# Six of sixteen gathered row tiles: gate on ScalarE, sum by accumulating DMA, in the combine of a mixture-of-experts layer

## The chip, the cores and the metric

The kernel is one program on one NeuronCore of a Trainium2 chip. The metric is the device time of one execution in microseconds (us), and the median of several executions is what counts. Five engines run their own instruction streams and meet only at semaphores: TensorE (PE), VectorE (DVE), ScalarE (ACT), GpSimd (POOL) and SyncE (SP). SP, ACT and POOL also issue DMAs.

## What is computed

One encoder layer over 512 tokens of width 1024: a mixer (convolution and neighbourhood attention, added to x to give h), then a mixture of experts, then a final RMSNorm. The change lies in the part of the experts in which their outputs are summed per token. Of the reference this matters:

```python
logits = (xt @ w_router + b_router).astype(jnp.float32)
top_vals, top_idx = lax.top_k(logits, TOP_K)          # TOP_K = 4 of 32 experts
gates = jax.nn.softmax(top_vals, axis=-1)
...                                                    # every expert's block of 128 rows: y
y = y * gate_pad[:, None]
out = jax.ops.segment_sum(y, tok_pad, num_segments=T)
h = h + out
return rmsnorm(h, g_final)
```

So each token's row of h receives four gated rows, one from each of its experts, and the final norm needs the finished row.

## The kernel before

The 512 tokens are four tiles n = 0 to 3 of 128 tokens. h stands in on-chip memory (SBUF) as 128 partitions x 4 tiles x 1024 floats.

The 32 experts run one after the other. An expert has 12 weight pieces of 1 MB (four each for gate, up and down). Each piece is split by ACT (`w_high`) and DVE (`w_low`) into two parts and used by 12 matmuls on PE (two k tiles, two halves, three products). Expert b's 128 output rows go to `y_rows` in DRAM by a DMA that ACT issues in `rows_out`. The last two experts (30 and 31, "late") don't go through DRAM: their gated rows are split into `late_high` (ACT, L849) and `late_low` (DVE, L1456), and PE places them in the four token tiles by one-hot matmuls (`open_tile`, `close_tile`, L1821 to L1833), whose sums stand in PSUM (`pair`).

The rows of the other experts come back as sixteen gathered row tiles, 128 x 1024 floats each. The four rows of a token are sorted by expert, so rank r = 0 is the row of the lowest expert. `row_order` is (r=0, n=0..3) as k = 0 to 3, and then for each n the ranks 1, 2, 3: k = 4 to 6 are tile 0, 7 to 9 tile 1, 10 to 12 tile 2, 13 to 15 tile 3. POOL gathers row tile k by an indirect DMA (L609) into one of nine buffers (`row_buf[k % 9]`), so row tile k of 9 and above waits until DVE has consumed row tile k - 9 (`combined`). DVE waits for the gather (`rows_back`, one of six semaphores) and does h[n] = row * gate + h[n] in one instruction (`add_row`, L1443).

Each engine's order is written out by hand; nothing reorders it:

- DVE in the end: the last weight split (`low_last`, L1206), `late_low` part 0, `add_row` 5 to 8, `late_low` part 1, `add_row` 9 to 15, then `add_late` for the four tiles (L1470: h[n] += PE's sum, after `late_summed`), then, after the norm's factor from POOL, the four final products (L1499).
- ACT in the end: `late_high` part 0, the last weight cast (L818), `late_high` part 1 (after PE's last piece), then the four squares with row sums (L927), each after its `add_late`.
- POOL in the end: the gathers in the order of k, then a branch on an overflow count (no trip is taken with these inputs), then for each tile two small instructions (L551, L553) that give the norm's factor.
- PE in the end: the last down pieces, three `open_tile`, then, after `late_low` part 1, three `close_tile` and tile 3's open and close.
- SP in the end: one output store of 512 KB per tile (L511), each after its final product, and a wait for all four.

Of the kernel before, what the change touches and what calls it, by code (L numbers as in the profile page):

```python
# [10 lines left out]
ALU = mybir.AluOpType  # L11
ACT = mybir.ActivationFunctionType
# [6 lines left out]
NQ = GRID_W // QB  # L19
# [4 lines left out]
N_EXPERTS, TOP_K, D_FF = 32, 4, 1024  # L24
# [17 lines left out]
NJ = NQ * TOP_K  # L42
# [15 lines left out]
def encoder_kernel(nc, x, g_mix, w_in, b_in, conv_w, conv_b, ln_g, ln_b, rpb, w_out, b_out,  # L58
# [3 lines left out]
    with ctx:  # L62
        def sem(name):
            return ctx.enter_context(nc.semaphore(name))
# [16 lines left out]
        def sb(name, shape, dt=F32):  # L81
            return area(name, shape, dt)[0]
# [5 lines left out]
        h = sb("h", [P, NQ, D_MODEL])  # L88
# [104 lines left out]
        row_order = [(0, n) for n in range(NQ)] + [(r, n) for n in range(NQ) for r in range(1, TOP_K)]  # L193
        row_buf = [xg] + [w_raw[i // 2][:, (i % 2) * D_MODEL:(i % 2 + 1) * D_MODEL] for i in range(8)]
        ROW_BUFS, ROW_SEMS = len(row_buf), 6
        y_sb = area_m[:, 1024:2048]
        bias_stage = area_m[:, 3072:4096]
        g_silu = area_t[0:CAP, 0:1024]
# [30 lines left out]
        slot_f, gate_of_rank, gate_extra = (area_t[:, 2128 + NJ * i:2128 + NJ * (i + 1)] for i in (1, 2, 3))  # L229
# [133 lines left out]
        late_high_ready = sem("late_high_ready")  # L363
        late_low_ready = sem("late_low_ready")
        late_summed = sem("late_summed")
        late_added = sem("late_added")
        bias_rows_loaded = sem("bias_rows_loaded")
        bias_high = sem("bias_high")
# [13 lines left out]
        rows_back = [sem(f"rows_back{k}") for k in range(ROW_SEMS)]  # L382
        extra_back = [sem(f"extra_back{n}") for n in range(NQ)]
        extra_added = sem("extra_added")
        combined = sem("combined")
# [130 lines left out]
        def _(pool):  # L516
# [60 lines left out]
            def select_in(e):  # L577
                g.tensor_copy(sel_gate[:, :], is_expert[:, bass.ds(e, 1)].to_broadcast([P, CAP]))  # L578
                g.tensor_copy(sel_up[:, :], is_expert[:, bass.ds(e + N_EXPERTS, 1)].to_broadcast([P, CAP])).then_inc(sel_in_ready, 1)
# [11 lines left out]
            with pool.Fori(0, N_EXPERTS - 2) as j:  # L591
                gather_next(j + 2)
                pool.wait_ge(piece_used, PIECES * j + 8 + UP + 1)
                select_in(j + 2)
            pool.wait_ge(ranks_ready, 1)
            for k, (r, n) in enumerate(row_order):
                if k == 0:
                    pool.wait_ge(y_stored, 16 * (LATE - 1 + 1))
                    pool.wait_ge(xg_transposed, N_EXPERTS)
                elif k < ROW_BUFS:  # L600
                    pool.wait_ge(piece_used, PIECES * (N_EXPERTS - 2) + 8 + GATE + (k - 1) // 2 + 1)
                else:
                    pool.wait_ge(combined, k - ROW_BUFS + 1)
                if k == NQ:
                    pool.wait_ge(y_stored, 16 * (LATE + 1))
                if k >= ROW_SEMS:
                    pool.wait_ge(rows_back[k % ROW_SEMS], 16 * (k // ROW_SEMS))
                i = n * TOP_K + r
                g.indirect_dma_start(out=row_buf[k % ROW_BUFS], out_offset=None, in_=y_rows[0:(LATE if r else LATE - 1) * CAP, :],  # L609
                                     in_offset=bass.IndirectOffsetOnAxis(ap=slot_of_rank[:, i:i + 1], axis=0)).then_inc(rows_back[k % ROW_SEMS], 16)  # L610
            pool.wait_ge(overflow_ready, 2)
            trips = pool.value_load(n_ovf[0:1, 0:1], min_val=0, max_val=MAX_OVERFLOW)
            with pool.If(trips > 0):
# [21 lines left out]
        def _(act):  # L635
            s = nc.scalar
# [94 lines left out]
            for i in range(1, NS + 7):  # L731
# [9 lines left out]
                n = turned_at(i, 2)  # L741
# [9 lines left out]
            for c in range(CC):  # L751
# [3 lines left out]
                             scale=colT[:, 24 + c:25 + c]).then_inc(silu_ready, 1)  # L755
# [82 lines left out]
            def rows_out(b, at, unstored=0):  # L838
# [4 lines left out]
                act.wait_ge(y_ready, b + 1 - unstored)  # L843
                act.dma_start(y_rows[bass.ds(b * CAP, CAP), :], y_sb[0:CAP, :]).then_inc(y_stored, 16)

            def late_high_part(i, at, of):

                act.wait_ge(piece_used, at)
                s.activation(late_high[i][:, :], of[:, :], ACT.Identity, scale=row_gate[:, i:i + 1]).then_inc(late_high_ready, 1)  # L849
# [53 lines left out]
            late_high_part(0, TAIL, pair[2])  # L903
            high_last(3, TAIL + 3)
            act.wait_ge(hT_low_ready, N_EXPERTS)
            late_high_part(1, EXTRA_BASE, pair[0])
            act.wait_ge(overflow_ready, 2)
            trips = act.value_load(n_ovf[0:1, 0:1], min_val=0, max_val=MAX_OVERFLOW)
            with act.If(trips > 0):
# [21 lines left out]
        def _(dve):  # L931
# [182 lines left out]
            for i in range(NS + 6):  # L1114
                n = normalised_at(i, 10)
# [6 lines left out]
                n = turned_at(i, 3)  # L1122
# [334 lines left out]
                                       ALU.mult, ALU.subtract).then_inc(late_low_ready, 1)  # L1457

            late_low_part(0, pair[2])
            for k in range(5, 9):  # L1460
                add_row(k)
            late_low_part(1, pair[0])
            for k in range(9, NJ):
                add_row(k)
            dve.wait_ge(combined, NJ)
            late_sum = [pair[1], pair[2], pair[3], pair[0]]

            def add_late(n):
                dve.wait_ge(late_summed, n + 1)
                v.tensor_tensor(h[:, n, :], h[:, n, :], late_sum[n][:, :], ALU.add).then_inc(late_added, 1)  # L1470

            for n in range(NQ):
                add_late(n)
            trips = dve.value_load(n_ovf[0:1, 0:1], min_val=0, max_val=MAX_OVERFLOW)
            with dve.If(trips > 0):
# [9 lines left out]
                for i in range(NJ):  # L1485
                    n = i // TOP_K
# [395 lines left out]
```

## Time and profile before

| | |
|---|---|
| Median of 3 runs | 1453.19 us (1452.91 to 1456.13) |
| The profiled execution | 1450.85 us |
| Its span, first to last instruction | 1448.9 us |
| PE busy | 1387.8 us (96%) |
| DVE busy | 1270.5 us (88%) |
| ACT busy | 966.5 us (67%) |
| POOL busy | 189.6 us (13%) |
| Mean granted TensorE clock | 0.980 of full speed |

All times "at 1421.79" are microseconds from the start of the span. A line of a timeline has the start, the duration, the engine, the line of the kernel, the operation, output<-input, and a count of instructions merged into the row; in brackets stands the idle time of the engine before it and what ended it. POOLq, SPq and ACTq are the sequencers of these engines, which issue DMAs. "To landing" is the time from the start of a DMA's issue until its semaphore is complete.

### The profile page before, as it was taken

To read this page: it belongs to the slowest core of one execution; us is meant where nothing else is said; L and a number is where in the kernel's file an instruction comes from. 1 tells how busy PE (TensorE), PEld (TensorE's weight loads), DVE (VectorE), ACT (ScalarE), POOL (GpSimd) and SP (SyncE) were. 2 spreads that over 40 slices of the span, in tenths; PEclk is the share of its full clock that TensorE was granted. 3 is DMA by queue.
4 is the path that set the end of the run, shared out by engine and by line. 5 is a ranking of instruction groups with operands and counts; after the bars stand their busy time and mean duration, and the time that the engine had idled before them with its cause. 6 is when DMAs were issued, how large, how long until landed. Compare 5 with 4: busy or idle time off the path is not lost.

```text
span 1448.9 us, 18708 instructions
## 1 busy us (share of the span) xinstructions
PE 1387.8 (96%) x6456; PEld 1146.7 (79%) x6456; DVE 1270.5 (88%) x996; ACT 966.5 (67%) x740; POOL 189.6 (13%) x191
## 2 busy tenths in 40 slices
PE   5999989799999999999999999999999999999994
PEld 4887767678888888888888888888888888888874
DVE  6899855899888888888888888888888888888898
ACT  3132643467777777777777777777777777777761
POOL 3000000011111111111111111111111111111062
PEclk9999789899999999999999999999999999999997
DMA  9922302799999999999999999999999999999983
GB/s 295 337 60 76 128 1 77 271 408 377 384 394 384 383 388 387 374 390 389 373 392 392 385 385 378 382 384 387 385 382 384 388 384 381 397 381 378 404 308 103
DMA packets 84978, 479.55 MB, mean 331 GB/s; under 512 B 10731, under 2 KB 11030, under 8 KB 35798
## 3 DMA queue, kind: packets, MB, share of 16 engines
q1 hardware_dynamic: 71982, 433.40, 76.8%
q0 software_dynamic: 6944, 25.18, 5.0%
q10 hardware_dynamic: 6024, 20.60, 3.6%
q8 instruction: 16, 0.26, 0.1%
q14 instruction: 12, 0.10, 0.0%
HBM read 449.82 MB, written 29.33 MB: 331 GB/s over the span
## 4 chain that ended last, share of the span: by engine, by line
PE 86%; DVE 9%; ACT 1%; issue 1%; DMA 1%; POOL 0%; SPq 0%; POOLq 0%; DVEq 0%; ACTq 0%
PE pair L1747 23%; PE pair L1745 23%; PE pair L1746 23%; DVE area_m L1016 2%; PE pair L1732 2%; PE pair L1725 2%; PE pair L1758 2%; PE pair L1530 2%; PE pair L1531 1%; PE pair L1532 1%; DVE w_low L1170 1%; DVE win_low L991 1%; DVE h L1443 1%; DMA h<-in_x 1%; PE pair L1611 1%
## 5 line engine op out<-in xcount | busy, mean ns | idle before, releaser
L1170 DVE TENSOR_TENSOR w_low<-w_raw,w_high 128x2048 fp32r<-128x2048 f32 x380 | 863.9, 2289 | 108.9 <-ACT w_high L774 105.8
L774 ACT CAST w_high<-w_raw 128x2048 fp32r<-128x2048 f32 x380 | 727.8, 1916 | 279.6 <-PE pair L1747 278.3
L1745 PE MATMUL pair<-w_high,xT_high 128*128 128x512 f32 x1008 | 395.1, 392 | 0.5 <-DVE xT_low L1228 0.5
L1747 PE MATMUL pair<-w_high,xT_low 128*128 128x512 f32 x1008 | 393.0, 390 | 0.0
L1746 PE MATMUL pair<-w_low,xT_high 128*128 128x512 f32 x1008 | 392.4, 389 | 0.0
L1747 PEld LDWEIGHTS pair<-w_high,xT_low 128*128 128x128 f32 x1008 | 189.2, 188 | 39.6
L1745 PEld LDWEIGHTS pair<-w_high,xT_high 128*128 128x128 f32 x1008 | 189.3, 188 | 39.2 <-DVE xT_low L1228 0.9
L1746 PEld LDWEIGHTS pair<-w_low,xT_high 128*128 128x128 f32 x1008 | 189.3, 188 | 38.4
L1745 PE MATMUL pair<-w_high,hT_high 128*128 128x512 f32 x496 | 195.8, 395 | 0.0
L1747 PE MATMUL pair<-w_high,hT_low 128*128 128x512 f32 x496 | 193.3, 390 | 0.0
L1746 PE MATMUL pair<-w_low,hT_high 128*128 128x512 f32 x496 | 193.3, 390 | 0.0
L578 POOL CAST sel_gate<-is_expert 128x128 fp32r (+1 forms) x32 | 34.6, 1082 | 669.3 <-PE pair L1747 669.3
L1747 PEld LDWEIGHTS pair<-w_high,hT_low 128*128 128x128 f32 x496 | 93.1, 188 | 19.6
L1746 PEld LDWEIGHTS pair<-w_low,hT_high 128*128 128x128 f32 x496 | 93.2, 188 | 18.5
L1745 PEld LDWEIGHTS pair<-w_high,hT_high 128*128 128x128 f32 x496 | 93.2, 188 | 18.4
L568 POOL DMA_INDIRECT area_m<-xn_rows,tok_now x32 | 81.4, 2544 | 38.2 <-issue 26.2
L1016 DVE SCALAR_TENSOR_TENSOR area_m<-area_u,convT,area_m 128x512 f32<-128x512 f32 x120 | 83.9, 752 | 0.4
L1532 PE MATMUL pair<-xnT_high,win_low 128*128 128x512 f32 x128 | 50.5, 394 | 0.0
L566 POOL COPY tok_now<-tok_tab 128x1 int32 (+1 forms) x31 | 17.1, 550 | 246.7 <-PE pair L1725 228.9
L1725 PEld LDWEIGHTS pair<-ident,area_m 128*128 128x128 f32 x256 | 33.6, 189 | 8.4 <-DMA area_m<-xn_rows,tok_now 6.0
L551 POOL TENSOR_SCALAR ms<-ss 128x1 f32<-128x1 f32 x12 | 5.8, 482 | 258.5 <-ACT area_t L789 239.7
L1725 PE MATMUL pair<-ident,area_m 128*128 128x128 f32 x256 | 34.3, 278 | 5.5 <-DMA area_m<-xn_rows,tok_now 5.5
(300 smaller groups left out, 1399.6 us busy)
## 6 DMA issues: line engine op xcount, KB each, us to landing
w_raw<-in_w_gate SPq DMA_DIRECT2D x128, 1024.0 KB, 7.0
w_raw<-in_w_up SPq DMA_DIRECT2D x128, 1024.0 KB, 6.5
w_raw<-in_w_down SPq DMA_DIRECT2D x128, 1024.0 KB, 7.0
y_rows<-area_m ACTq DMA_DIRECT2D x30, 512.0 KB, 7.6
ring<-in_w_in SPq DMA_DIRECT2D x5, 2048.0 KB, 17.7
y_rows<-area_t SPq DMA_DIRECT2D x1, 8704.0 KB, 37.0
ring<-in_w_out SPq DMA_DIRECT2D x2, 2048.0 KB, 8.5
h<-in_x SPq DMA_DIRECT2D x4, 512.0 KB, 8.7
```

The costliest lines, as they stand in the source:

```text
L568: g.indirect_dma_start(out=xg[0:CAP, :], out_offset=None, in_=xn2_rows, in_offset=bass.IndirectOffsetOnAxis(ap=tok_now[:, 0:1], axis=0)).t ...
L578: g.tensor_copy(sel_gate[:, :], is_expert[:, bass.ds(e, 1)].to_broadcast([P, CAP]))
L774: s.copy(w_high[:, i % HIGH_RING, :], w_raw[i][:, :]).then_inc(high_ready, 1)
L1016: v.scalar_tensor_tensor(mixedT[:, c, :], u_pad[:, c, k:k + SEQ], convT[:, k * CC + c:k * CC + c + 1], mixedT[:, c, :], ALU.mult, ALU.add) ...
L1170: v.tensor_tensor(w_low[i][:, :], w_raw[i][:, :], w_high[:, i % HIGH_RING, :].bitcast(F32), ALU.subtract).then_inc(low_ready, 1)
L1530: t.matmul(to, a_high, b_high, start=(k == 0 and not opened), stop=False)
L1532: return t.matmul(to, a_low, b_high, start=False, stop=(k == KD - 1))
L1725: last = t.transpose(bank[6 + k // 4][:, (k % 4) * CAP:(k % 4 + 1) * CAP], xg[0:CAP, k::KD], ident[0:CAP, 0:CAP])
L1732: last = t.transpose(bank[6 + k // 4][:, (k % 4) * CAP:(k % 4 + 1) * CAP], h_tok[:, k::KD], ident[0:CAP, 0:CAP])
L1745: t.matmul(to[half], tok_high, hi, start=(opens and kk == 0), stop=False)
L1746: t.matmul(to[half], tok_high, lo, start=False, stop=False)
L1747: last = t.matmul(to[half], tok_low, hi, start=False, stop=(k == KD - 1))
```

## The change

Row tiles k = 10 to 15 (`DMA_ROWS` = 10: ranks 1 to 3 of token tiles 2 and 3) leave DVE. ACT waits for each one's gather and multiplies the buffer by its gates in place (`gate_row_of`); 10 and 11 stand before `late_high` part 1, 12 to 15 behind it. POOL then issues one accumulating DMA for each, from the row buffer into h[n], both in SBUF (`add_by_dma`). The three accumulating DMAs of one tile wait for one another, since each reads and rewrites the same bytes of h. In POOL's order they stand so: gather 13, add 10, gather 14, add 11, gather 15, add 12, add 13, add 14, add 15. On DVE `late_low` part 1 moves ahead of row tile 8, rows 8 and 9 follow it, and the `add_late` of tiles 2 and 3 wait until their three accumulating DMAs have landed.

```diff
+        DMA_ROWS = NQ + 2 * (TOP_K - 1)
...
+        row_gated = sem("row_gated")
+        rows_added = [sem(f"rows_added{n}") for n in range(2)]
...
+            def add_by_dma(k):
+
+                r, n = row_order[k]
+                pool.wait_ge(row_gated, k - DMA_ROWS + 1)
+                if r > 1:
+                    pool.wait_ge(rows_added[n - 2], 16 * (r - 1))
+                pool.dma_start(h[:, n, :], row_buf[k % ROW_BUFS], accum_op=ALU.add).then_inc(rows_added[n - 2], 16)
...
                 g.indirect_dma_start(out=row_buf[k % ROW_BUFS], out_offset=None, in_=y_rows[0:(LATE if r else LATE - 1) * CAP, :],
                                      in_offset=bass.IndirectOffsetOnAxis(ap=slot_of_rank[:, i:i + 1], axis=0)).then_inc(rows_back[k % ROW_SEMS], 16)
+                if k >= DMA_ROWS + TOP_K - 1:
+                    add_by_dma(k - (TOP_K - 1))
+            for k in range(DMA_ROWS + TOP_K - 1, NJ):
+                add_by_dma(k)
             pool.wait_ge(overflow_ready, 2)
...
+            def gate_row_of(k):
+
+                i = row_order[k][1] * TOP_K + row_order[k][0]
+                act.wait_ge(rows_back[k % ROW_SEMS], 16 * (k // ROW_SEMS + 1))
+                s.activation(row_buf[k % ROW_BUFS], row_buf[k % ROW_BUFS], ACT.Identity,
+                             scale=gate_of_rank[:, i:i + 1]).then_inc(row_gated, 1)
...
             act.wait_ge(hT_low_ready, N_EXPERTS)
+            for k in range(DMA_ROWS, DMA_ROWS + 2):
+                gate_row_of(k)
             late_high_part(1, EXTRA_BASE, pair[0])
+            for k in range(DMA_ROWS + 2, NJ):
+                gate_row_of(k)
...
             late_low_part(0, pair[2])
-            for k in range(5, 9):
+            for k in range(5, 8):
                 add_row(k)
             late_low_part(1, pair[0])
-            for k in range(9, NJ):
+            for k in range(8, DMA_ROWS):
                 add_row(k)
-            dve.wait_ge(combined, NJ)
+            dve.wait_ge(combined, DMA_ROWS)
             late_sum = [pair[1], pair[2], pair[3], pair[0]]
 
             def add_late(n):
                 dve.wait_ge(late_summed, n + 1)
+                if n >= 2:
+                    dve.wait_ge(rows_added[n - 2], 16 * (TOP_K - 1))
                 v.tensor_tensor(h[:, n, :], h[:, n, :], late_sum[n][:, :], ALU.add).then_inc(late_added, 1)
```

## Rows read from the trace of the kernel before

**Rows 1.** The page: busy time by engine, and shares of the chain that ended last.
```profile
PE 1387.8 (96%) x6456; PEld 1146.7 (79%) x6456; DVE 1270.5 (88%) x996; ACT 966.5 (67%) x740; POOL 189.6 (13%) x191
...
PE 86%; DVE 9%; ACT 1%; issue 1%; DMA 1%; POOL 0%; SPq 0%; POOLq 0%; DVEq 0%; ACTq 0%
```
**Rows 2.** Timeline of DVE, the tail.
```profile
1411.64 4.51 DVE L1206 TENSOR_TENSOR w_low<-w_raw,w_high 128x2048 fp32r<-128x2048 f32 x2
1416.07 1.28 DVE L1456 SCALAR_TENSOR_TENSOR late_low<-pair,small,late_high 128x1024 fp32r<-128x1024 f32 x1
1417.27 5.44 DVE L1443 SCALAR_TENSOR_TENSOR h<-w_raw,area_t,h 128x1024 f32<-128x1024 f32 x4
1422.94 1.28 DVE L1456 SCALAR_TENSOR_TENSOR late_low<-pair,small,late_high 128x1024 fp32r<-128x1024 f32 x1 [0.24 <-ACT late_high L849]
1424.14 1.27 DVE L1443 SCALAR_TENSOR_TENSOR h<-area_m,area_t,h 128x1024 f32<-128x1024 f32 x1
1425.52 8.23 DVE L1443 SCALAR_TENSOR_TENSOR h<-w_raw,area_t,h 128x1024 f32<-128x1024 f32 x6
1433.78 4.61 DVE L1470 TENSOR_TENSOR h<-h,pair 128x1024 f32<-128x1024 f32 x4
1438.32 2.47 DVE L1499 SCALAR_TENSOR_TENSOR w_raw<-h,rstd,area_a 128x1024 f32<-128x1024 f32 x2
...
1443.23 1.28 DVE L1499 SCALAR_TENSOR_TENSOR w_raw<-h,rstd,area_a 128x1024 f32<-128x1024 f32 x1 [0.72 <-POOL rstd L553]
```
**Rows 3.** Timeline of PE: ends of tile 0's and tile 3's sums.
```profile
1426.29 0.39 PE L1832 MATMUL pair<-late_low,late_1h 128*128 128x512 f32 x1
...
1430.37 0.39 PE L1832 MATMUL pair<-late_low,late_1h 128*128 128x512 f32 x1
```
**Rows 4.** Timeline of ACT, the tail.
```profile
1411.93 1.90 ACT L818 CAST w_high<-w_raw 128x2048 fp32r<-128x2048 f32 x1
1421.79 1.12 ACT L849 ACTIVATE late_high<-pair,small 128x1024 fp32r<-128x1024 f32 x1 [7.96 <-PE pair L1747]
1435.04 1.06 ACT L927 ACTIVATE area_t<-h 128x1024 f32<-128x1024 f32 x1 [12.13 <-DVE h L1470]
...
1438.76 1.06 ACT L927 ACTIVATE area_t<-h 128x1024 f32<-128x1024 f32 x1
```
**Rows 5.** Timeline of POOL: the last three gathers, and the norm factors of tiles 2, 3.
```profile
1411.99 2.74 POOL L609 DMA_INDIRECT w_raw<-y_rows,slot_of_rank  x1 [9.12 <-DVE h L1443]
1418.81 1.93 POOL L609 DMA_INDIRECT w_raw<-y_rows,slot_of_rank  x1 [4.08 <-DVE h L1443]
1421.05 1.08 POOL L609 DMA_INDIRECT w_raw<-y_rows,slot_of_rank  x1 [0.30 <-issue]
...
1438.76 0.89 POOL L551 TENSOR_SCALAR ms<-ss 128x1 f32<-128x1 f32 x1 [0.41 <-ACT area_t L927]
1439.73 1.47 POOL L553 TENSOR_TENSOR rstd<-ms,small 128x1 f32<-128x1 f32 x1
1441.28 1.29 POOL L551 TENSOR_SCALAR ms<-ss 128x1 f32<-128x1 f32 x1
```
**Rows 6.** DMA view, window 1411 to 1418.4 (queue: packets, MB, share of 16 engines; landing).
```profile
q0 software_dynamic: 152, 0.54, 24.1%
...
w_raw<-y_rows,slot_of_rank POOLq DMA_INDIRECT x1, 6.1
```
**Rows 7.** DMA view, windows of the gathers issued at 1418.81 and 1421.05: landing.
```profile
w_raw<-y_rows,slot_of_rank POOLq DMA_INDIRECT x1, 5.1
...
w_raw<-y_rows,slot_of_rank POOLq DMA_INDIRECT x1, 5.5
```
**Rows 8.** Windows view, one stretch: engines busy, clock, DMA share, GB/s.
```profile
1411.50:1412.00 0.50, 0.50 (x3) 0.40 (x3) 0.50 (x2) 0.50 (x2) 0.01 (x1) 1.00 0.00 0
```
**Rows 9.** Landing of all sixteen gathers (L609).
```profile
DMA to landing us min/median/max: 5.0/9.3/13.6
```
**Rows 10.** Landing of the four output stores (L511).
```profile
DMA to landing us min/median/max: 3.7/4.0/4.1
```

## Prediction

> **What bounds the kernel now.** I read the page first: PE is busy for 96% of the span and holds 86% of the chain that ended last [rows 1]. The change touches none of PE's work, so it can pay only after PE's last matmul. I then read the tail engine by engine. PE finishes tile 0's sum at 1426.7 (1426.29 + 0.39) and tile 3's at 1430.76 [rows 3]. DVE is later than that: after `late_high` part 1 (ACT, 1421.79 to 1422.91 [rows 4]) it does `late_low` part 1, then seven rows from 1424.14 to 1433.75, then four `add_late` to 1438.39 [rows 2]. ACT's last square waits for the last of these and starts at 1438.76 [rows 4]; POOL's small instructions follow, slow from 1438.76 on while DVE runs its final products [rows 5]; the last product ends at 1444.51 [rows 2], and its store of about 4.0 us [rows 10] ends the span at 1448.9. So behind PE's last matmul DVE is the bound: tile 3's `add_late` starts at about 1437.2 (start 1433.78, fourth of four at 1.15 us), 6.4 us after its PE sum was there. From its start to the end of the span are 11.7 us. The span is 1448.9, the profiled execution 1450.85, 2.3 us below the median of 1453.19; I add the change in the span to the median.
>
> **What is removed.** Six `add_row` leave DVE. Six took 8.23 us [rows 2], 1.39 us each with the wait between them. With them gone, row 8 and row 9 follow `late_low` part 1 (1424.2) and end at 1426.9; `add_late` of tile 0 can start at once, since PE's sum for it came at 1426.7 [rows 3]. Tile 1 follows at 1428.2. If nothing else held it, tile 3 would start with PE at 1430.9: 6.3 us earlier. That is the whole prize.
>
> **What is added on ACT.** Six activations of a 128x1024 tile. The nearest rows are 1.12 us (from PSUM with a scale) and 1.06 us (from SBUF) [rows 4]; I take 1.1. Gates 10 and 11 stand after the last weight cast, which ends at 1413.83 [rows 4], so they run to about 1416.1. ACT then idled for 7.96 us until 1421.79 [rows 4], so these two are free and `late_high` part 1 isn't late. They need gathers 10 and 11: the DMA engines stand idle at 1411.5 [rows 8] with everything issued before, gather 12 included, landed. Without that cover each would cost 1.1 us of the path through `late_high`. Gates 12 to 15 run from 1422.9, 1.1 us apart, gates 14 and 15 not before their gathers; none is later than the POOL queue needs it, below.
>
> **What is added on POOL and the DMA queue, where the end now hangs.** Write D for the time from the end of an accumulating DMA's issue to its landing. The order on POOL is: gather 13, add 10, gather 14, add 11, gather 15, adds 12 to 15. Adds 11 and 12 wait for the landing of the one before (same tile), 14 and 15 likewise, and 13, although it waits for no add, stands behind 12 in POOL's order. So five landings follow one another on the way to the end: 10, 11 (then 12 and 13 are issued back to back), 13, 14 and 15, and 15 must have landed before tile 3's `add_late`. What is queued behind each waiting add on POOL: gather 14 behind add 10, gather 15 behind add 11, the norm factors of all four tiles behind add 15.
>
> The issue cost: gathers took 2.74 us while DVE ran L1206, 1.93, and 1.08 us [rows 5, 2]. I take 1.9 for add 10 (DVE is busy) and 1.0 for the others, when DVE mostly waits.
>
> D isn't in the trace: there is no accumulating DMA in it, nor any transfer from SBUF to SBUF. Bounds: the same 512 KB as a gather landed 6.1 us after a 2.74 us issue on idle DMA engines, so D = 3.4, and 5.1 - 1.93 = 3.2 for the next; one that went behind another took 5.5 - 1.08 = 4.4 [rows 5 to 7]. That is the lower bound, 3.2, with 1.2 more behind another transfer. An accumulate must read h as well as the row, twice the reading: one gather held all 16 DMA engines for 24.1% of 7.4 us = 1.78 us [rows 6]; the same once more gives D = 5.0. The upper bound is the median gather among weight loads, 9.3 us less a 1.9 us issue, D = 7.4 [rows 5, 9]. I take 5.0, since the engines are otherwise idle there and the second read has to go somewhere.
>
> In sentences that the rest can do without: the Trainium skill (Collectives: The Full Stack, The bandwidth ceiling) says that a reducing transfer is about half as fast as a copy because the add needs two source reads, not because the add itself takes cycles; no transfer in this trace adds, so the trace can't say. 
>
> **The sum**, with D = 5.0 and 0.1 us for a wake:
> - add 10: gate 10 is done at 1415.0, issue 1415.3 to 1417.2, lands 1422.2.
> - gather 14 as before, 1418.81. Add 11: 1422.3 to 1423.3, lands 1428.3. Gather 15 follows: 1423.6 to 1424.9, lands about 1429.7, gate 15 at 1430.9.
> - add 12: 1428.4 to 1429.4, lands 1434.4 (tile 2's `add_late` then, hidden).
> - add 13: 1429.7 to 1430.7, behind add 12 in the queue (+1.2), lands 1436.9.
> - add 14: 1437.0 to 1438.0, lands 1443.0. Add 15: 1443.1 to 1444.1, lands 1449.1.
> - tile 3's `add_late`: 1449.1 to 1450.3. DVE's final products of tiles 0 to 2 stand behind it: to 1454.1. Meanwhile the square ends at 1451.6 and POOL's pair for tile 3 takes between 0.8 and 2.8 us [rows 5]: 1452.5 to 1454.5. POOL's factors for tiles 0 to 2 were done during add 15's flight, which before they were not; that saves some 0.6 us of the 11.7. The last product starts at about 1454.4, ends at 1455.7, and with 4.4 us of store and end as before (1444.51 to 1448.9) the span is 1460.1.
>
> That is 11.2 us more than 1448.9: 1462.05 for the profiled execution, and on the median 1453.2 + 11.2 = **1464.4 us**.
>
> **Rivals.**
> 1. The accumulate costs no more than a copy (D = 3.2). Then add 11 is issued behind gather 14, 1421.05 to 1422.05, lands 1425.3; add 12 to 1427.3 (DVE busy with row 9, 1.9 us), lands 1430.5; add 13 lands at 1433.0, add 14 at 1437.3, add 15 at 1441.6. Tile 3 starts 4.4 us later than now, less 0.6, gives +3.7: 1456.9. With issues of 0.8 us and no queueing behind add 12 it would be about +2.2: 1455.4. For it: landing times are mostly fixed cost (3.2 us against 1.78 us of engine time). Against it: the doubled reading.
> 2. The accumulate is slow, D = 7.4 or more. The same sum gives landings at 1424.6, 1433.1, 1441.6, 1444.1 (13), 1452.6 and 1461.1; +23.2, 1476.4. For it: nothing but that no such transfer is seen; against it: idle DMA engines [rows 8].
> 3. Faster: DVE's relief is collected. The mechanism is a transfer within SBUF, with no DRAM at either end, landing much sooner than a gather. It breaks even where tile 3's last add lands at 1437.8 and gains more than 0.3% where it lands before 1433.4; from add 10's issue end at 1417.2 five links and four issues of 1 us must fit in 16.2 us, so D below about 2.2, against 3.2 for the fastest gather and 3.7 - 0.55 (the store's own issue) for the fastest store [rows 10]. At the limit, PE's 1430.9, the span falls by 6.3 + 0.6 us: 1446.3.
> 4. The edit does nothing to the end because another wait hides it: ACT's gates make `late_high` late, or the adds of both tiles run side by side. The first is excluded by 7.96 us of idle; the second by POOL's order. What is left of it is case 1.
>
> **How the numbers follow.** Chances: forecast (D between about 3.7 and 6.5, +4.5 to +19) 0.58; rival 1, 0.22; rival 2, 0.15; faster, 0.04; no effect by another way, 0.01. A measurement of this kernel tells about 0.3% (4.4 us) from no change. Rival 1 is mostly just within that, so: slower 0.78, same 0.18, faster 0.04. The range takes in rival 1's copy-priced sum and reaches to D = 7.4: 1455.5 to 1477.
>
> **What would show it.** In the changed kernel's trace: no `add_row` after about 1427 and DVE idle before the `add_late` of tile 2 and, longest, of tile 3; PE unchanged to 1430.8 (if PE's end moves, my reading of ACT's idle time is wrong); POOL idle four or five times for several us, each ended by the landing of an accumulating DMA; their landing from the start of issue near 6 us (4.2 if rival 1 holds, 8.4 or more if rival 2); the q0 queue's engine time up by six transfers of about 3.5 us. After the last landing some 11 us to the end. The prediction is wrong if adds land within 3 us of their issue, if tile 3's chain doesn't start behind tile 2's last issue, or if the landing isn't what ends DVE's wait.

## The result and the profile after

The changed kernel takes 1461.27 us (median of 6 runs, 1460.64 to 1462.83) against 1453.05 us (6 runs, 1451.91 to 1456.13) of the kernel before, measured together: a ratio of 1.0053 with a 95% interval of 1.0040 to 1.0066, 8.2 us slower. The forecast was 1464.4 us in a range of 1455.5 to 1477.

The profiled execution's span is 1459.0 us, 10.1 us over that of before. The page of the changed kernel, busy time by engine, where [rows 1] stood: PE's work is the same, DVE has six instructions less, ACT and POOL six more each.

```profile
PE 1387.9 (95%) x6456; PEld 1146.3 (79%) x6456; DVE 1263.1 (87%) x990; ACT 972.6 (67%) x746; POOL 193.6 (13%) x197
```

The timeline of DVE in the tail answers [rows 2] (line numbers have moved: L1469 is `add_row`, L1482 `late_low`, L1498 `add_late`, L1527 the final products).

```profile
1424.68 1.28 DVE L1482 SCALAR_TENSOR_TENSOR late_low<-pair,small,late_high 128x1024 fp32r<-128x1024 f32 x1 [1.56 <-ACT late_high L871]
1425.88 1.27 DVE L1469 SCALAR_TENSOR_TENSOR h<-w_raw,area_t,h 128x1024 f32<-128x1024 f32 x1
1427.26 1.28 DVE L1469 SCALAR_TENSOR_TENSOR h<-area_m,area_t,h 128x1024 f32<-128x1024 f32 x1
1428.58 2.35 DVE L1498 TENSOR_TENSOR h<-h,pair 128x1024 f32<-128x1024 f32 x2
1434.74 1.22 DVE L1498 TENSOR_TENSOR h<-h,pair 128x1024 f32<-128x1024 f32 x1 [3.80 <-DMA h<-w_raw]
1447.34 1.22 DVE L1498 TENSOR_TENSOR h<-h,pair 128x1024 f32<-128x1024 f32 x1 [11.38 <-DMA h<-w_raw]
1448.58 3.68 DVE L1527 SCALAR_TENSOR_TENSOR w_raw<-h,rstd,area_a 128x1024 f32<-128x1024 f32 x3
1452.69 1.28 DVE L1527 SCALAR_TENSOR_TENSOR w_raw<-h,rstd,area_a 128x1024 f32<-128x1024 f32 x1 [0.44 <-POOL rstd L556]
```

DVE is done with its rows at 1428.5, does `add_late` of tiles 0 and 1, and then stands idle for 3.80 us before tile 2's and 11.38 us before tile 3's, each time until an accumulating DMA into h has landed. The 8.2 us that six `add_row` took are off DVE, and 15.2 us of waiting have come in. Who makes DVE wait stands in POOL's timeline (L604 is the accumulating DMA, L620 the gather; it answers [rows 5]).

```profile
1412.61 2.74 POOL L620 DMA_INDIRECT w_raw<-y_rows,slot_of_rank  x1 [9.89 <-DVE h L1469]
1416.98 1.00 POOL L604 DMA_DIRECT2D h<-w_raw  x1 [1.63 <-ACT w_raw L865]
1420.62 2.03 POOL L620 DMA_INDIRECT w_raw<-y_rows,slot_of_rank  x1 [2.64 <-DVE h L1469]
1422.61 1.01 POOL L604 DMA_DIRECT2D h<-w_raw  x1
1423.93 1.03 POOL L620 DMA_INDIRECT w_raw<-y_rows,slot_of_rank  x1 [0.30 <-issue]
1429.16 1.88 POOL L604 DMA_DIRECT2D h<-w_raw  x2 [4.21 <-DMA h<-w_raw]
1437.63 0.87 POOL L604 DMA_DIRECT2D h<-w_raw  x1 [6.60 <-DMA h<-w_raw]
1442.70 0.87 POOL L604 DMA_DIRECT2D h<-w_raw  x1 [4.21 <-DMA h<-w_raw]
```

Add 10 goes at 1416.98, add 11 at 1422.61, 12 and 13 back to back at 1429.16, 14 at 1437.63, 15 at 1442.70. Three of these waits end with the landing of an add: 12 waits for 11, 14 for 13, 15 for 14. The chain that ended last, in order of time (start, duration, what), is in its last 25 us before the tail nothing but these landings:

```profile
1422.61 5.99 DMA h<-w_raw
...
1429.76 7.33 DMA h<-w_raw
...
1437.63 4.54 DMA h<-w_raw
...
1442.70 4.55 DMA h<-w_raw
...
1447.34 1.23 DVE h L1498
```

The last two stand alone on the queue: 4.54 and 4.55 us from the start of the issue to the landing. The 7.33 us are add 13's, which was issued 0.6 us behind add 12, while that one was under way.

**Why the two profiles differ by 10.1 us and the medians by 8.2.** PE's last matmul starts at 1432.17 in the changed kernel, 1.8 us later than [rows 3] has it. The granted clock makes up most of it (1.6 us), and the rest was there at the start of the experts. The windows view (engines busy, then the granted clock, DMA share, GB/s), one line of before, then two of the changed kernel:

```profile
1406.00:1408.00 2.00, 2.00 (x11) 1.64 (x10) 1.55 (x2) 2.00 (x2) 0.00 (x0) 1.00 1.02 410
```

```profile
1404.00:1406.00 2.00, 1.65 (x9) 1.65 (x10) 2.00 (x2) 0.00 (x0) 0.00 (x0) 0.72 0.98 393
1406.00:1408.00 2.00, 2.00 (x6) 1.52 (x6) 1.44 (x2) 2.00 (x2) 0.00 (x0) 0.50 1.03 408
```

In both, PE has been idle for 2.8 us before it goes on at 1404.2 and 1404.4. In the profile of before the clock then stayed at 1.00 (2.4 GHz), in that of the changed kernel it fell to 0.50 (1.2 GHz) for some 3.5 us. From the last weight cast on ACT before that idle time to `late_high` part 1 are 23.0 us in before and 24.6 us in the changed kernel. The change isn't what makes it fall. The second profile of the order with two chains (below) has all six accumulating DMAs and a clock that stays at 1.00 behind the same idle time, with 22.9 us for the same distance:

```profile
1408.00:1410.00 2.00, 2.00 (x13) 1.74 (x13) 1.89 (x2) 1.33 (x2) 0.23 (x1) 1.00 1.01 416
```

The profiles of the other ten runs below show the fall and 24.4 to 24.6 us, two of them of kernels without any of the six DMAs. So that neither the start nor the clock touches them, the experiments are read by a distance: from the start of `late_high` part 1 on ACT (it starts with PE's last piece) to the start of tile 3's `add_late` on DVE. Before: 1421.79 to 1437.2, 15.4 us [rows 2, 4]. Changed: 1423.53 to 1447.34, 23.8 us. The difference, 8.4 us, agrees with the 8.2 us of the medians.

### The profile page after: what moved, and what is told of

Read it like the earlier page. It is cut to its first block, busy times and chain, and to the rows that moved or that the text cites. A ratio compares the mean times of both kernels' runs of the same rounds, so it can differ in the third digit from the quotient of the medians.

```text
span 1459.0 us, 18714 instructions
## 1 busy us (share of the span) xinstructions
PE 1387.9 (95%) x6456; PEld 1146.3 (79%) x6456; DVE 1263.1 (87%) x990; ACT 972.6 (67%) x746; POOL 193.6 (13%) x197
## 4 chain that ended last, share of the span: by engine, by line
PE 81%; DVE 9%; SPq 4%; DMA 3%; issue 1%; ACT 1%; POOL 0%; POOLq 0%; DVEq 0%; ACTq 0%
PE pair L1775 23%; PE pair L1773 23%; PE pair L1774 23%; DVE area_m L1042 3%; SPq L457 2%; PE pair L1760 2%; PE pair L1753 2%; PE pair L1786 2%; DMA h<-w_raw 2%; DVE w_low L1196 1%; SPq L447 1%; DMA h<-in_x 1%; DVE win_low L1017 1%; PE pair L1639 1%; DVE ring L1063 1%
## 5 line engine op out<-in xcount | busy, mean ns | idle before, releaser
L1773 PEld LDWEIGHTS pair<-w_high,hT_high 128*128 128x128 f32 x496 | 93.7, 189 | 18.5
L1774 PEld LDWEIGHTS pair<-w_low,hT_high 128*128 128x128 f32 x496 | 93.5, 189 | 18.6
L1370 DVE SCALAR_TENSOR_TENSOR area_q<-area_t,area_q 128x1024 f32<-128x1024 f32 x32 | 38.9, 1217 | 0.1
```

Source lines behind the costliest of these rows:

```text
L1370: v.scalar_tensor_tensor(h_tok, g_silu, SILU_TOP, u_lim, ALU.min, ALU.mult).then_inc(h_tok_ready, 1)
L1773: t.matmul(to[half], tok_high, hi, start=(opens and kk == 0), stop=False)
L1774: t.matmul(to[half], tok_high, lo, start=False, stop=False)
```

## The experiments

The theory: the end hangs on accumulating DMAs that wait for one another, each landing some 4.5 us or more (five in a row by the forecast; the chain shows four, 11, 13, 14 and 15); ACT's gates and the reordering on DVE cost nothing. The rivals: the cost is in the bytes or the load on the queue, in ACT's gates, in DVE's new order, or in contention.

### A plain copy in place of the accumulate

```diff
-                pool.dma_start(h[:, n, :], row_buf[k % ROW_BUFS], accum_op=ALU.add).then_inc(rows_added[n - 2], 16)
+                pool.dma_start(h[:, n, :], row_buf[k % ROW_BUFS]).then_inc(rows_added[n - 2], 16)
```

> The changed kernel with the six accumulating DMAs made plain copies: h's tiles 2 and 3 are overwritten by the gated row, so the sum over a token's four rows is left out there. Order, waits and bytes of the row buffers stay. Theory (five landings in a row set the end, and an accumulate is dearer than a copy because it reads h as well): in the changed kernel's trace a lone accumulate took 4.54 us from the start of its issue to its landing, of which the DMA engines moved data for about 2.8 us; a gather of the same bytes held them 1.8 us. A copy should land in about 3.6 us, 0.9 to 1.0 us sooner, and with five links the span should fall by 4.5 to 5 us: +3 to +4 us over the kernel before. Rival (fixed cost of issue and landing, the reading doesn't matter): landing stays at 4.5 us and the time at +8 us.

Measured: 1456.98 us against 1453.33, ratio 1.0024 (1.0014 to 1.0034), +3.6 us. A lone copy lands in 2.88 us, sooner than the 3.6 us expected. The DMA view of the window around the lone transfer of add 14 (queue: packets, MB, share of 16 engines; landing), first the accumulate in the changed kernel (window of 4.9 us), then the copy (3.4 us):

```profile
q0 software_dynamic: 144, 0.52, 56.4%
...
h<-w_raw POOLq DMA_DIRECT2D x1, 512.0 KB, 4.5
```

```profile
q0 software_dynamic: 144, 0.52, 38.0%
...
h<-w_raw POOLq DMA_DIRECT2D x1, 512.0 KB, 2.9
```

The accumulate holds the 16 engines for 56.4% of 4.9 = 2.76 us, the copy for 38.0% of 3.4 = 1.29 us: 2.1 times as long for the same bytes. The issue is shorter too, 0.54 against 0.87 us. So the accumulation is part of a link's price. The Trainium skill (Collectives: The Full Stack, The bandwidth ceiling) says of the reducing step of a collective that it is half as fast as a copy because the add needs two source reads. The ratio of 2.1 agrees, though these runs can't tell the second read from the addition itself.

That the time came out as expected is in part luck. The two lone links shortened by 1.66 us each, add 11's and 13's by 0.8 and 1.0, together 5.1 us. Copy 13, issued behind copy 12, still took 6.29 us to land. In its last 2.9 us the queue moved hardly anything (window 1432.8 to 1435.7):

```profile
q0 software_dynamic: 15, 0.05, 5.0%
```

What holds up the last packets of a transfer issued right behind another stays open.

### Half the columns

```diff
-                pool.dma_start(h[:, n, :], row_buf[k % ROW_BUFS], accum_op=ALU.add).then_inc(rows_added[n - 2], 16)
+                pool.dma_start(h[:, n, 0:HALF], row_buf[k % ROW_BUFS][:, 0:HALF], accum_op=ALU.add).then_inc(rows_added[n - 2], 16)
```

> The changed kernel with the accumulating DMAs on columns 0 to 511 only: the additions of the other half of the columns are left out for these six row tiles. Theory (each link is a fixed part of about 1.8 us, issue included, and 2.8 us of moving data that halves with the bytes): a lone link falls from 4.54 us to about 3.2 us, five links by 6.5 to 7 us, so the time is +1 to +2 us over before. Rival (fixed cost per descriptor or per DMA): links stay above 4.2 us and the time at +7 us or more. If DVE's or PE's own tail took over as the bound, the fall would stop at about -1 us relative to before; it should not come to that.

Measured: 1455.76 us, ratio 1.0013 (1.0003 to 1.0023), +2.4 us; a lone link takes 3.30 us. 256 KB less save 1.24 us, so, if the time goes in a straight line with the bytes, a link of 4.54 us is 2.5 us that go with them and 2.1 us that don't. The lone link came out as expected. The total is 0.4 to 1.4 us above it because five links were counted, and the chain has four. The timeline of POOL:

```profile
1422.86 1.02 POOL L604 DMA_DIRECT2D h<-w_raw  x1
1424.17 1.03 POOL L620 DMA_INDIRECT w_raw<-y_rows,slot_of_rank  x1 [0.30 <-issue]
1428.32 1.87 POOL L604 DMA_DIRECT2D h<-w_raw  x2 [3.11 <-ACT w_raw L865]
```

From add 11's issue to add 12's are 5.5 us, against 6.6 in the changed kernel: 1.1 us less. (The row names ACT as the releaser, but gate 12 was done by 1426.0; by the kernel's waits it was add 11's landing, which is under way together with gather 15 at its full size.) Add 13's landing falls from 7.33 to 5.59 us. With 1.24 us for each of the two lone links the sum is 1.1 + 1.7 + 2.5 = 5.3 us, and the distance from `late_high` to `add_late` falls by as much.

### ACT's gates alone

```diff
+            for k in range(DMA_ROWS, DMA_ROWS + 2):
+                gate_row_of(k)
             late_high_part(1, EXTRA_BASE, pair[0])
+            for k in range(DMA_ROWS + 2, NJ):
+                gate_row_of(k)
...
+                if k >= DMA_ROWS:
+                    dve.wait_ge(row_gated, k - DMA_ROWS + 1)
+                    v.tensor_tensor(h[:, n, :], row_buf[k % ROW_BUFS], h[:, n, :], ALU.add).then_inc(combined, 1)
+                    return
```

> The kernel before with ScalarE's part of the change alone: ACT multiplies row tiles 10 to 15 by their gates, DVE then adds them with a plain add instead of multiply and add. Theory (ACT's part is hidden in its 8 us of idle time and only the DMAs cost): DVE's six adds keep the 1.28 us or fall to 1.2 us each, the time is -0.5 to 0 us of before, and late_high part 1 starts where PE's last piece ends. Rival (the gates hold up late_high part 1 or arrive later than DVE wants them): the time rises by 1 to 3 us, with DVE idle ahead of its adds.

Measured: 1452.46 us, ratio 0.9989 (0.9979 to 0.9999), -0.9 us. ACT's timeline:

```profile
1415.96 2.20 ACT L852 ACTIVATE w_raw<-w_raw,area_t 128x1024 f32<-128x1024 f32 x2
1423.97 1.12 ACT L858 ACTIVATE late_high<-pair,small 128x1024 fp32r<-128x1024 f32 x1 [5.81 <-PE pair L1764]
```

The first two gates take 2.2 us of ACT's idle time, and 5.81 us of it are left before `late_high`, which still waits for PE. The gates are free, and DVE's plain adds come at a pitch of 1.30 instead of 1.37 us.

### DVE's new order alone

```diff
-            for k in range(5, 9):
+            for k in range(5, 8):
                 add_row(k)
             late_low_part(1, pair[0])
-            for k in range(9, NJ):
+            for k in range(8, NJ):
                 add_row(k)
```

> The kernel before with the one step of the change that moves no work: VectorE does late_low part 1 ahead of row tile 8. Theory (the reordering is neutral for the end, since DVE does the same instructions and is the bound behind PE's last matmul): DVE waits about 1.5 us for late_high part 1 with row 8 not yet done, so up to 1.4 us later at the end, 0 to +1.5 us. In the changed kernel that wait is harmless, since its end hangs on the DMAs. Its trace also shows whether TensorE's granted clock falls after the 2.8 us gap at 1401 to 1404 in a kernel with no accumulating DMA: if it does, the 1.6 us by which all later work was late in the changed kernel's profile is no effect of the change; the rival is that only kernels with the change show it.

Measured: 1454.11 us against 1453.56, ratio 1.0009 (0.9998 to 1.0020): no difference that can be told, and in the trace the distance from `late_high` to `add_late` is 1.4 us longer, from the 1.62 us that DVE waits for `late_high`. Its windows view shows the fall of the clock (0.59 over these 2 us) with no accumulating DMA in the kernel:

```profile
1406.00:1408.00 2.00, 2.00 (x7) 1.57 (x7) 1.08 (x2) 1.88 (x2) 0.00 (x0) 0.59 1.02 404
```

### Two chains side by side

The six row tiles are taken as rank 1 of tiles 2 and 3, rank 2 of both, rank 3 of both. The bytes are the same, but each chain has three links and they run beside each other.

```diff
-        row_order = [(0, n) for n in range(NQ)] + [(r, n) for n in range(NQ) for r in range(1, TOP_K)]
+        row_order = [(0, n) for n in range(NQ)] + [(r, n) for n in range(2) for r in range(1, TOP_K)] + [(r, n) for r in range(1, TOP_K) for n in (2, 3)]
```

> The changed kernel with the last six row tiles taken in the order rank 1 of tiles 2 and 3, rank 2 of both, rank 3 of both, so that each accumulate waits for the one before the last and the two tiles' chains run side by side. The same six transfers and bytes. Theory (serial landings cost, not bytes): by the links measured, adds 10 to 15 land at about 1421, 1426, 1430, 1432, 1435.5 and 1438.5 on the time axis of the kernel before, the last add_late starts some 1 to 2 us later than before, and the time is +0.5 to +2.5 us over before, 6 to 7 us better than the change. Rival (the cost is the load on the DMA queue or on SBUF, since the bytes are the same): as the change, +8 us. Second rival (tile 3's chain now starts early but gather 15, held behind add 11, arrives late): gather 15 lands after 1429 and the last add waits for its gate, +4 us.

Measured: 1458.71 us (7 runs), ratio 1.0031 (1.0018 to 1.0044), +5.4 us: above what was expected, while the distance in the trace (1423.11 to 1441.22 = 18.1 us) said +2.7. So both kernels were measured once more, together.

> The two-chain order once more, since its first measurement (+2.6 to +6.4 us over before) was above what was expected of it and didn't agree with its own profiled execution (span +2.8 us once the late PE is taken off). Theory A (serial landings only, the first estimate): +0.5 to +2.5 us. Theory B (landings side by side lengthen each other, since both transfers want all 16 DMA engines; links of 5.0 to 7.0 us in its chain of work instead of 4.5 us): +3 to +5 us, still 3 to 5 us under the change. Rival (bytes alone count): the same as the change.

> The changed kernel itself, beside the two-chain order on the same chip, so that the two are compared with the same runs of before. Theory: +7 to +9 us over before, as on the first measurement; the lone accumulates of tile 3 take 4.5 us again. A drift of the chip would show here as another distance.

Measured: the two chains 1455.83 us (11 runs) against 1453.94, ratio 1.0014 (1.0005 to 1.0023), +1.9 us; the changed kernel 1461.92, ratio 1.0058 (1.0046 to 1.0071), +8.0 us as before. The second distance of the two chains is 18.3 us (1425.05 to 1443.38), +2.9. The intervals of the two measurements overlap only at 1.0018 to 1.0023; I take the traces' +2.8 us.

The traces show one thing that can part two measurements so far. The stream of experts doesn't start at the same time in every execution. Before any changed instruction, the first ACT cast of `xT_high` behind 335 us starts at 336.2 in the first profile of the two chains (1455.16 us) and at 339.6 in the second (1457.24 us). Of the first measurement's seven executions three lie at 1455.2 to 1455.7 and four at 1458.7 to 1460.5. Whether those four started late isn't shown, since only the profiled one has a trace.

Either way the same six transfers in another order cost 2 to 5 us and not 8, so neither bytes nor load on the queue make the change's loss; the rival falls. The chain that ended last of the second profile:

```profile
1418.50 5.44 DMA h<-w_raw
...
1424.13 6.23 DMA h<-w_raw
...
1430.91 6.99 DMA h<-w_raw
...
1438.43 4.86 DMA h<-w_raw
```

Side by side a link takes 5 to 7 us instead of 4.5: what is gained by fewer links is partly lost again. That is what the first estimate had left out; between the two theories of the second run the measurement doesn't decide (+1.9 is nearer the first, the links are the second's).

### One tile by DMA

Tile 2 alone goes by DMA, DVE takes row tiles 13 to 15 again.

```diff
-            for k in range(DMA_ROWS + TOP_K - 1, NJ):
-                add_by_dma(k)
...
-            for k in range(8, DMA_ROWS):
+            for k in (8, 9, 13, 14, 15):
                 add_row(k)
```

> The changed kernel with tile 2 alone by accumulating DMA (row tiles 10 to 12); VectorE takes 13 to 15 again. Theory (a chain of landings costs nothing while it ends before DVE's own rows): three links, the last landing at about 1433 on the axis of before; DVE's rows end 4.2 us earlier than before at 1429.6, its add_late of tile 2 waits 1 us for the landing, tile 3's starts 3 us earlier than before. Time -1.5 to -3.5 us. Rival (accumulating DMAs cost in themselves, by contention with DVE's or ACT's accesses to SBUF): instructions of DVE get longer and the time is no better than before.

Measured: 1451.02 us, -2.5 us by the medians, ratio 0.9990 (0.9979 to 1.0002), which just includes no change; the distance in the trace is 2.7 us shorter. In that trace three links cost DVE no wait at all:

```profile
1428.56 4.06 DVE L1466 SCALAR_TENSOR_TENSOR h<-w_raw,area_t,h 128x1024 f32<-128x1024 f32 x3
1432.65 4.61 DVE L1495 TENSOR_TENSOR h<-h,pair 128x1024 f32<-128x1024 f32 x4
```

DVE goes from its last row straight into four `add_late`, at the durations it has without such DMAs (4.06 for three rows, 1.28 each). Add 12 is issued at 1429.35 and is under way beside these rows. So here an accumulating DMA doesn't slow DVE; it costs only when somebody waits.

### One row of each tile, early

If a landing costs only where it is waited for, the rows for the DMAs should be ones whose landing nobody needs: rank 1 of tiles 1, 2 and 3, one link each. They are gathered as k = 5 to 7, ACT gates them in its idle time ahead of `xT_high` (4.7 us before), and POOL issues them behind gather 12, when it idled for 9.1 us until gather 13 [rows 5].

```diff
+                if k == ROW_BUFS + NQ - 1:
+                    for t in range(1, NQ):
+                        pool.wait_ge(row_gated, t)
+                        pool.dma_start(h[:, t, :], row_buf[NQ + t], accum_op=ALU.add).then_inc(rows_added[t], 16)
...
                     if last and i == DOWN + 2:
+                        for k in range(NQ + 1, 2 * NQ):
+                            gate_row_of(k)
                         hT_high_part(N_EXPERTS - 1, xT_high)
...
+                if r == 2 and n:
+                    dve.wait_ge(rows_added[n], 16)
```

> A new arrangement: three row tiles by ScalarE and accumulating DMA, but one each of tiles 1, 2 and 3 (rank 1), gathered as k = 5 to 7, gated in ACT's idle time at 1401 to 1405, added while POOL idles before gather 13, so that no add waits for another and all are down before VectorE comes to these tiles. Theory (what costs is a landing that somebody waits for): VectorE's tail is three rows of 1.39 us shorter, nobody waits for an add; last add_late 4 us earlier, time -3 to -4.5 us: about 1449.5. Rival (beside weight loads the adds take 8 to 12 us and gather 14 and 15, which now wait for the adds' buffers, come late; or the gates hold up ACT's xT_high and so PE): time within 1 us of before or worse.

Measured: 1449.17 us against 1453.56, ratio 0.9974 (0.9962 to 0.9985), -4.4 us. The adds land only after 11.9 to 13.7 us, beside weight loads and gathers, and nobody waits for them:

```profile
DMA to landing us min/median/max: 11.9/13.3/13.7
```

```profile
1426.63 5.43 DVE L1462 SCALAR_TENSOR_TENSOR h<-w_raw,area_t,h 128x1024 f32<-128x1024 f32 x4
1432.09 4.61 DVE L1489 TENSOR_TENSOR h<-h,pair 128x1024 f32<-128x1024 f32 x4
```

### Five and four rows

In five rows, rank 2 of tiles 2 and 3 follows, issued behind gather 15. In four, only rank 2 of tile 1 does, issued as soon as tile 1's first add has landed, ahead of gathers 14 and 15.

```diff
+                if k == ROW_BUFS + NQ:
+                    pool.wait_ge(row_gated, NQ)
+                    pool.wait_ge(rows_added[1], 16)
+                    pool.dma_start(h[:, 1, :], row_buf[8], accum_op=ALU.add).then_inc(rows_added[1], 16)
```

> As the arrangement with one row each of tiles 1, 2 and 3, and rank 2 of tiles 2 and 3 as well, gated where the change gates its first two, added right behind gather 15. Five row tiles leave VectorE. Theory: VectorE's six last rows end at about 1427, tiles 0 to 2 follow PE's sums, and tile 3's add_late starts with PE's last sum at 1430.9: the bound goes back from VectorE to PE, 6.3 us earlier than before, and the last product is bound by the square and POOL's two instructions as before; time -5 to -6.5 us: about 1447.5. Rival: the second adds land after 1426 and VectorE waits for them before rank 3 of tiles 2 and 3: -3 us at best, no better than three rows.

> One row each of tiles 1, 2 and 3 added early while POOL idles, as in the arrangement that gave -4.4 us, and a fourth (rank 2 of tile 1) gated by ACT before late_high part 1 and issued as soon as the first add of tile 1 is down, ahead of gathers 14 and 15. Theory: VectorE's tail is one row (1.4 us) shorter again; time -5 to -6 us. Rival (as in the arrangement with five rows, where ACT's gate stood 2.7 us on a late gather ahead of xT_high and the second adds landed 9 us after their issue): gathers 14 and 15, issued behind the wait for the first add, come after VectorE wants them, or the gate holds up PE; then it is no better than three rows, -2 to -4.4 us.

Measured: five rows 1452.68 us, ratio 0.9987 (0.9975 to 0.9999), -0.9 us; four rows 1447.97 us (5 runs) against 1453.94, ratio 0.9965 (0.9952 to 0.9978), -6.0 us (-5.1 by the ratio). That is the lowest of all, though by the intervals it isn't clear of three rows; in the traces its distance is 1.1 us shorter. In five, DVE waits again for landings, and ACT stands on a gather ahead of `xT_high` (two lines of DVE and two of ACT, from their timelines):

```profile
1431.13 1.28 DVE L1470 SCALAR_TENSOR_TENSOR h<-w_raw,area_t,h 128x1024 f32<-128x1024 f32 x1 [2.71 <-DMA h<-w_raw]
1433.58 1.28 DVE L1470 SCALAR_TENSOR_TENSOR h<-w_raw,area_t,h 128x1024 f32<-128x1024 f32 x1 [1.16 <-DMA h<-area_m]
...
1408.75 1.15 ACT L862 ACTIVATE w_raw<-w_raw,area_t 128x1024 f32<-128x1024 f32 x1 [2.65 <-DMA w_raw<-y_rows,slot_of_rank]
1409.81 1.00 ACT L881 ACTIVATE xT_high<-pair 128x1024 fp32r<-128x1024 f32 x1
```

The first is the forecast's mechanism in small: 3.87 us of waits, more than the two rows saved. The second costs PE nothing that shows. `late_high` part 1 starts at 1425.99, 4.2 us later than in before, but 2.7 us of this are there long before, at the cast that starts at 336.27 in before and here at

```profile
338.93 1.01 ACT L885 CAST xT_high<-pair 128x1024 fp32r<-128x1024 f32 x1
```

and from the last weight cast ahead of PE's idle time to `late_high` part 1 are 24.6 us, as in the other kernels whose clock fell, with such a wait or without. In four rows ACT waits for the same gather (2.63 us), with 24.5 us for that distance. Of the twelve executions with five rows three lie at 1447.8 to 1448.8 and nine, the profiled one among them, at 1452.1 to 1453.8. So the median says little of this arrangement; that late starts part the two groups isn't shown. In four rows DVE's tail has no wait:

```profile
1426.24 4.04 DVE L1469 SCALAR_TENSOR_TENSOR h<-w_raw,area_t,h 128x1024 f32<-128x1024 f32 x3
1430.31 4.62 DVE L1496 TENSOR_TENSOR h<-h,pair 128x1024 f32<-128x1024 f32 x4
```

### All of them by one yardstick

The yardstick is the start of `late_high` part 1 to the start of tile 3's `add_late` (where four `add_late` stand in one row, its start and three pitches of 1.15 us), and its difference to the 15.4 us of before; beside it the difference of the medians, each to before measured with it. It leaves out both the start of the experts and the clock behind PE's idle time.

| kernel | yardstick, us | to before | medians |
|---|---|---|---|
| changed, first and again | 23.8, 23.8 | +8.4 | +8.2, +8.0 |
| two chains, first and again | 18.1, 18.3 | +2.7, +2.9 | +5.4, +1.9 |
| plain copy | 18.6 | +3.2 | +3.6 |
| half the columns | 18.5 | +3.1 | +2.4 |
| late_low first | 16.8 | +1.4 | +0.6 |
| gates only | 15.0 | -0.4 | -0.9 |
| one tile | 12.7 | -2.7 | -2.5 |
| five rows | 12.4 | -3.0 (experts started 2.7 us late) | -0.9 |
| three rows | 11.3 | -4.1 | -4.4 |
| four rows | 10.2 | -5.2 | -6.0 |

## Why the prediction was right, step by step

- **What bounds the kernel** was right: with rows off DVE and no wait in their place the end comes earlier (three and four rows), by 1.3 to 1.4 us for each row in the traces and 1.5 by the medians. (8.23 us for six rows are 1.37 each, not 1.39.)
- **ACT's gates are free**: right, 1.10 us each, 5.8 us of idle time left ahead of `late_high` part 1.
- **Five landings in a row**: right in kind, wrong by one. The end does hang on a chain of landings, but of four: 11, 13, 14, 15. Add 10's is not among them: by the time POOL came to add 11, behind gather 14, it had landed, which with the forecast's D of 5.0 it would not have. With two chains instead of one the loss goes from 8 to between 2 and 5 us.
- **The size of a link** is the term that was mis-sized. I took D = 5.0 us from the end of the issue to the landing; it was 4.54 - 0.87 = 3.7. Two errors lie in it. I started from a gather, 3.2 us, but the nearest thing is a copy within SBUF, which no row of before showed: 2.88 - 0.54 = 2.3. And I added 1.78 us for the second read, where accumulate and copy differ by 3.7 - 2.3 = 1.3. That D is double-priced in transfer was right (2.76 against 1.29 us of engine time); it was doubled from the wrong base. The Trainium skill (DMA: Bandwidth & Descriptors, Anatomy of one DMA) gives 2.0 us plus bytes over 436 GB/s for a DMA on the GpSimd path, an estimate of 3.2 us for each of these three. Counted from the end of the issue, as D is, it fits the gather, is 0.9 us too much for the copy and 0.5 us too little for the accumulate.
- **Shared links**: I gave add 13, behind add 12, 1.2 us more; its landing took 7.33 us against 4.54, 2.8 us more. That is as much as the engine time of one accumulate, but a whole transfer doesn't explain it in the plain copy, which has 1.29 us of engine time and takes 6.29 us against 2.88, 3.4 us more. What does stays open. This error went the other way.
- **A wake of 0.1 us** was too little: from a landing to the next issue are 0.53 us (1437.10 to 1437.63 in the chain), so a lone link costs 4.54 + 0.53 = 5.1 us where the sum had 6.1.
- **The sum** put the last landing at 1449.1; it came at 1447.25, and less the 1.8 us of the late PE at 1445.4, 3.7 us before the forecast. Add 11 started 1.5 us sooner (1422.61 - 1.8 against 1422.3), from add 14's issue to add 15's landing were 9.6 us instead of 12.1, and from add 11's issue to add 14's 15.0 instead of 14.7: 1.5 + 2.5 - 0.3 = 3.7. With 0.7 us more behind it, the forecast's 11.2 us become the 8.2 that were measured.
- **The end behind it**: I took 11.0 us from tile 3's `add_late` to the end, 0.6 less than before; it was 11.7 (1447.34 to 1459.0), no saving. POOL's factors for tiles 0 to 2 were done early, as said, but its last two small instructions ran at 1.27 and 1.47 us beside DVE's final products, and DVE waited 0.44 us for them:

```profile
1449.83 1.27 POOL L554 TENSOR_SCALAR ms<-ss 128x1 f32<-128x1 f32 x1 [3.40 <-ACT area_t L953]
1451.19 1.47 POOL L556 TENSOR_TENSOR rstd<-ms,small 128x1 f32<-128x1 f32 x1
```

- **Forecast against rivals**: a D of 3.7 lies at the lower edge of the forecast's case (3.7 to 6.5), nearer to rival 1's 3.2 than to 5.0, and by the sign put down beforehand the lone landing of 4.54 us is nearer to rival 1's 4.2 than to 6. For D = 3.7 the prediction gives +4.5 us, and 8.2 were measured. The missing 3.7 us are mainly those of the shared links: from add 11's issue to add 14's its sum has 12.1 us with that D (14.7 less two times 1.3), and 15.0 were measured; 0.7 more are the end. So the mechanism was right, but that the time lies only 3 us from the forecast is in part luck, a link priced too dear against shared landings priced too cheap. Rival 1's time (+3.7) is what the plain copy gave (+3.6), though by another path: its copy lands sooner (2.3 us against 3.2), and its shared link takes longer. Rival 3 (faster) had named transfers within SBUF as the mechanism; they are faster than a gather, but not below the 2.2 us that it needed.

## What to carry to other kernels

Before work is moved from an engine to accumulating DMAs, count the landings that wait for one another: on one tile they are a chain, and here a link cost 5.1 us and more where VectorE did the same addition in 1.4 us. Put one transfer on each of several tiles, early, where its landing is nobody's wait; then even 12 to 14 us to landing cost nothing, and each row was worth 1.3 to 1.5 us. Compare traces by a distance that begins behind whatever differs between executions: here the start of the experts and the clock moved the end by up to 3.5 and 1.6 us. Look also at what stands behind the waiting DMA in the issuing queue: tile 3's chain was late because it stood behind tile 2's.

## What the runs showed of the hardware

- A 512 KB accumulate within SBUF from GpSimd: 4.54 us from issue start to landing alone, 2.76 us of it on all 16 engines; a plain copy 2.88 and 1.29 us; 256 KB accumulated 3.30 us. The issue takes 0.87 us for the accumulate and 0.54 us for the copy.
- Two accumulates issued within 1 us: the second lands after 7.3 us; with plain copies after 6.3 us. Issued beside weight loads, accumulates landed after 10.4 to 13.7 us.
- TensorE's granted clock fell from 1.00 to 0.50 after an idle time of 2.8 us in eleven of thirteen profiles, with and without accumulating DMAs, and stayed at 1.00 after the same 2.8 us in two: that of before, and one of two of the two-chain order. The fall cost 1.5 to 1.6 us. What decides it in an execution stays open.
